# Side products of two feed-forwards: from behind a step's up products to ahead of them

## The reference, cut to what matters

```python
def conv_ffn(h, w_up, conv_w, conv_b, w_down):
    u = causal_dwconv(h @ w_up, conv_w, conv_b)
    g, up = jnp.split(u, 2, axis=-1)
    return (jax.nn.silu(g) * up) @ w_down
```

## Time and profile before

| | us |
|---|---|
| median of 3 runs | 2046.79 (2045.48 to 2047.96) |
| the profiled execution, its time | 2051.6 |
| its span | 2049.8 |
| PE busy | 2009.4 (98%) |
| DVE busy | 1330.0 (65%) |
| ACT busy | 955.7 (47%) |
| POOL busy | 159.3 (8%) |
| mean granted TensorE clock | 0.996 |

### The profile page before, as it was taken

One profiled execution on the slowest core, in us unless ns is written; L12 is line 12 of the kernel. 1 busy time (PEld: TensorE's weight loads), 2 busy tenths in 40 slices (PEclk: granted clock), 3 DMA queues, 4 the chain that ended last, 5 costly groups with the idle time before them and its releaser, 6 DMA issues.

```text
span 2049.8 us, 33452 instructions
## 1 busy us (share of the span) xinstructions
PE 2009.4 (98%) x13114; PEld 1738.3 (85%) x13114; DVE 1330.0 (65%) x2339; ACT 955.7 (47%) x1574; POOL 159.3 (8%) x169
## 2 busy tenths in 40 slices
PE   9999999999999999999999999999999999999998
PEld 7779998878999888888888788888878899888997
DVE  6767667767877337476445555868566686575665
ACT  4655555565555434353432453233246454445444
POOL 2001000000110100000200001111110000100100
PEclk9999999999999999999999999999999999999999
DMA  8446665535555322222222104534234244441554
GB/s 248 148 142 245 228 225 196 181 108 175 186 176 191 137 93 81 75 83 83 72 93 93 52 31 157 193 116 161 92 129 154 93 135 155 134 154 57 193 172 134
DMA packets 79706, 285.54 MB, mean 139 GB/s; under 512 B 8976, under 2 KB 9644, under 8 KB 79552
## 3 DMA queue, kind: packets, MB, share of 16 engines
q1 hardware_dynamic: 71136, 256.93, 37.7%
q10 hardware_dynamic: 6416, 19.51, 2.7%
q0 software_dynamic: 2000, 6.97, 1.3%
HBM read 277.55 MB, written 5.83 MB: 138 GB/s over the span
## 4 chain that ended last, share of the span: by engine, by line
PE 81%; DVE 10%; ACT 6%; issue 2%; DMA 1%; POOL 0%; ACTq 0%; DVEq 0%; SPq 0%
PE pb L1124 16%; PE pb L1126 15%; PE pb L1125 15%; PE pb L1137 6%; PE pb L1139 6%; PE pb L1138 6%; DVE SPL L2222 3%; ACT SPH L1637 3%; PE pb L1143 3%; PE pb L1302 2%; PE pb L1496 2%; PE pb L1303 2%; PE pb L1304 2%; PE pb L1477 2%; PE pb L1391 1%
## 5 line engine op out<-in xcount | busy, mean ns | idle before, releaser
L2222 DVE TENSOR_TENSOR SPL<-RAW,SPH 128x1024 fp32r<-128x1024 f32 x460 | 558.9, 1232 | 367.2 <-ACT SPH L1637 343.4
L1637 ACT ACTIVATE SPH<-RAW 128x1024 fp32r<-128x1024 f32 x462 | 477.4, 1052 | 208.4 <-PE pb L1126 111.3
L1124 PE MATMUL pb<-HTH,SPH 128*128 128x256 f32 (+1 forms) x1304 | 447.0, 343 | 8.4 <-POOL HTL L2881 3.1
L1126 PE MATMUL pb<-HTH,SPL 128*128 128x256 f32 (+1 forms) x1304 | 437.9, 336 | 0.0
L1125 PE MATMUL pb<-HTL,SPH 128*128 128x256 f32 (+1 forms) x1304 | 437.5, 335 | 0.0
L1124 PEld LDWEIGHTS pb<-HTH,SPH 128*128 128x128 f32 x1304 | 247.8, 190 | 36.8 <-ACT HTH L1686 3.2
L1126 PEld LDWEIGHTS pb<-HTH,SPL 128*128 128x128 f32 x1304 | 247.8, 190 | 26.1
L1125 PEld LDWEIGHTS pb<-HTL,SPH 128*128 128x128 f32 x1304 | 248.0, 190 | 24.8
L1137 PE MATMUL pb<-SPH,HTH 128*128 128x512 f32 x640 | 254.6, 398 | 2.1 <-DVE SPL L2222 1.4
L1139 PE MATMUL pb<-SPL,HTH 128*128 128x512 f32 x640 | 249.9, 390 | 0.0
L1138 PE MATMUL pb<-SPH,HTL 128*128 128x512 f32 x640 | 249.8, 390 | 0.0
(11 more groups left out here) (297 smaller groups left out, 2853.2 us busy)
## 6 DMA issues: line engine op xcount, KB each, us to landing
RAW<-in_w_up SPq DMA_DIRECT2D x88, 512.0 KB, 4.5
RAW<-in_wa SPq DMA_DIRECT2D x64, 512.0 KB, 3.5
RAW<-in_w_in SPq DMA_DIRECT2D x48, 512.0 KB, 4.7
RAW<-in_wmg SPq DMA_DIRECT2D x48, 512.0 KB, 3.5
RAW<-in_wbr SPq DMA_DIRECT2D x48, 512.0 KB, 3.5
RAW<-in_w_down SPq DMA_DIRECT2D x44, 512.0 KB, 4.9
RAW<-in_w_ada SPq DMA_DIRECT2D x24, 512.0 KB, 4.7
ARAW<-in_w_ada ACTq DMA_DIRECT2D x24, 512.0 KB, 4.2
```

Source lines behind the costliest of these rows:

```text
L1124: T.matmul(o, wh[:, kt, :], xh[:, kt, n0:n1], start=kt == 0, stop=False)
L1126: m = T.matmul(o, wl[:, kt, :], xh[:, kt, n0:n1], start=False, stop=kt == 7)
L1637: A.activation(hi, raw, ACT.Copy, scale=1.0).then_inc(*act.tick(s["hi"], ("u", u)))
L2222: W.tensor_tensor(lo, raw, hi.bitcast(F32), SUB).then_inc(*dve.tick(s["lo_dve"], ("u", u)))
```

## The change

In layer 0 one item of the modulation is taken at the head of steps 2 to 19, ahead of the up products, instead of behind the up products of steps 1 to 18. In layer 1 one product of the context is taken at the head of steps 8 to 15 instead of behind the up products of steps 7 to 14. ScalarE, behind its three DMAs and ahead of its wait for them, waits for VectorE's tile of ones and copies one column of it into a scratch tile.

```diff
         for j in range(FF_TILES + 2):
+            if l == 0 and 2 <= j < 20:
+                next(self.ada)
+            if l == 1 and 8 <= j < 16:
+                next(context)
             if j < FF_TILES:
...
                 self.add("up", l, j)
                 self.give(n)
-            if l == 0 and 1 <= j < 19:
-                next(self.ada)
             if j == 1 and l == 0:
...
                 context = self.products("c0", LO4)
-            if 7 <= j < 15 and l == 1:
-                next(context)
             if j == 3 and l == 1:
...
         A.dma_start(sb["PAR"][:, FIRST_PAR:], k.args["par"][:, FIRST_PAR:]).then_inc(*act.tick(s["par2"]))
+        act.wait_ge(s["const_dve"], "one")
+        A.activation(sb["SQY"][:, 0:1], sb["ONE"][:, 0:1], ACT.Copy, scale=1.0).then_inc(*act.tick(s["const_act"]))
         act.wait_ge(s["par"], 32)
```

## The result

The change made the kernel slightly slower: 2048.93 us (median of 22 runs, 2043.92 to 2053.63) against 2045.43 (22 runs, 2043.52 to 2048.28) for the kernel before. The ratio is 1.0014, with an interval of 1.0008 to 1.0020, or 1.6 to 4.1 us. I had forecast 3.5 us less.

The account below looks back on a forecast made before the run. The prediction took TensorE as the bound, 81% of the chain that ended last. Modulation -3.0, context -0.45 and tiny copy 0 made -3.5 from the runs' median 2046.8, so 2043.3 us, range 2040.0 to 2047.6.

Parts of the forecast that it names:

- The context: Second feed-forward: 8 products moved between downs and ups, each 0.44 instead of 0.50 at the slow pace; -0.45 us in all.
- hidden: VectorE's two context operations ahead of the step's splits, wanted 8.8 us later and taking 2.3, would cost TensorE nothing.
- The paces: Ups run at one of two stable paces, 276 or 281 ns per matmul, 0.20 us apart over a block of 48.
- both products give the fast pace: Rival: ups behind context products also run fast, so the context gives -2.1 and the total is 2041.7; chance 0.20.
- The modulation: First feed-forward: moved products and turns, with fast ups behind the products, give -3.0 us in all.
- turns: First feed-forward: 3 moved turns, each 0.69 at the fast pace instead of 0.93, counted at 0.23 gain each, -0.69.
- the stretch up to step 5: First feed-forward, three products included: -0.4 with a 0.6 wait for a split; bounds -1.1 and +0.6.
- its bound without a wait: The modulation's stretch up to step 5 if nothing waits: -1.1 instead of -0.4.
- The rival of late up loads: Loads landing after more than 5.1 us would delay evacuation, 1.3 in each of 11 steps: 2057; chance 0.08.
- the 1.5 to spare: First feed-forward: the next down unit would be split at 13.0, TensorE wanting it at 14.5, so 1.5 us spare.
- ScalarE's tiny copy: At the start: table load 1.28 us earlier, but TensorE still meets the first split unit at 13.26; 0, bounds -1.3 and +0.2.
- something not seen: Anywhere in the kernel: paces of later blocks shift by some 2 us in sum; chance 0.05.

Follow-up runs that it names:

- e9_mid: Against the kernel before, only the context: TensorE's product ahead of the ups, other engines' work between that step's up splits and evacuation; second feed-forward 193.9 us.
- e4: Against the kernel before, only TensorE's context products move ahead of the ups of steps 7 to 14, other engines' work stays; ratio 0.9982.
- e6: The changed kernel, but the other engines' work on the context product put back behind that step's evacuation; 2040.93 us, ratio 0.9970 to the kernel before.
- e1_mod: Against the kernel before, only the modulation's products move; ratio 0.9987.
- e7: As e6, with ScalarE's four table loads issued in step 10 of the first feed-forward instead of step 3; ratio 0.9968 to the kernel before.
- e8: As e7, with the context rows loaded in step 7 instead of 1 and spilled in step 13 instead of 6; ratio 0.9966 to the kernel before.
- e3_tiny: Against the kernel before, only ScalarE's tiny copy is added; ratio 0.9996.
- e12_mod: Against the kernel before, only the modulation's products move, run once for its trace; first feed-forward 194.8 us, second 190.0.
- e2_ctx: Against the kernel before, only the context's products move; ratio 1.0020.
- e10: The changed kernel again, nothing altered, run once for its trace; first feed-forward 195.2 us, second 194.7.
- e11: The changed kernel once more, nothing altered, run once for its trace; first feed-forward 194.5 us, second 194.7.
- e5: Against the kernel before, TensorE's context product stays behind the ups, only the other engines' work on it moves to the next step's head; ratio 1.0023.

## Why the prediction was wrong, by its own steps

**The context, the term that failed.** The prediction said that VectorE's two operations "now stand ahead of the splits of the step. These are wanted a whole step (8.8) later and take 2.3: hidden", and put the move at -0.45. It came to +4.5, where TensorE's own steps got shorter: the term failed at "hidden". Two things were missed. I added up VectorE's operations as if nothing stood between them; between them is a copy of ScalarE's, and behind that copy on ScalarE's queue stand the up units' splits. And the lead of a step was taken for slack that is there each time. It is used up once: the first two products show no wait, the third 0.16, and from then on every round is 9.64 long and the step too. The rows of the ring were all in the trace of before; what I didn't do was to walk them in the new order and set the sum against the 8.81 that I forecast for the step (8.65 where TensorE doesn't wait). e9_mid shows that such a sum can be made beforehand, once the ring is known: 9.56 against 9.54. The prediction named its own end: it falls if the two feed-forwards together don't become 1 to 6 us shorter. They became 3.4 longer.

**The paces.** The prediction took the fast pace behind the modulation's products (right: 5.57 against 5.56) and the slow one behind the context's, by the earlier trace rows (wrong: fast in all eight, 5.55 where the block is undisturbed). So of the rivals, *both products give the fast pace* was the true one as far as TensorE goes: its -2.1 for the context is e4's 188.2 against 190.0 to 190.2. The earlier trace rows was the wrong neighbour in two ways. Ahead of that product stand ups, not downs; and the pace there is not the place's own. In eleven of the fourteen profiled executions these ups are fast, in three slow (the kernel before, e4, e6), in each at the pace of the ups ahead of the products. In the changed kernel five starts take 0.57 instead of 0.59:

```profile
1549.17 0.28 PE L1125 MATMUL pb<-HTL,SPH 128*128 128x256 f32 x1
...
1549.74 0.28 PE L1124 MATMUL pb<-HTH,SPH 128*128 128x256 f32 x1
```

For the modulation's product, e1_mod answers what the prediction could not read: there the ups ahead of the first product were slow (11.50 for two blocks instead of 11.10), and the ups behind it fast (5.56).

**The modulation, the second term that failed.** It was put at -3.0 and came to -1.14. The paces and seams were right: steps of 8.97 with a product against 8.94 forecast, turns about 0.2 cheaper (0.23 forecast). What was wrong is the stretch up to step 5, forecast at -0.4 with a wait of 0.6 in it and +0.6 as the worst. It came to +1.15 in the profiled execution (40.73 instead of 39.58), with waits of 2.01. Less these waits the loop is 193.5, 3.15 under the kernel before; the sum at its bound without a wait was -3.7.

**The rival of late up loads** was right in kind and put too far off. It was to decide at a landing of 5.1; by the table above it decides near 3.7 in step 4. The difference is the 1.42 for which ScalarE issues the table loads, of the kind that I had in the earlier trace rows and had not taken off the 1.5 to spare in this rival. That is worked out from rows, and e7 and e8 agree: with the table loads in step 10 the downs of step 11 wait at landings of 3.93 and 3.86. Behind all other products of the second and third group no downs waited.

**ScalarE's tiny copy**, at 0: nothing is to be seen of it. The table load is at 2.17, the first matmul with a split unit at 13.51 (13.26 before), and e3_tiny's interval includes 1. Over all profiled executions that first matmul is at 12.4 to 13.7 with the copy and at 12.5 to 13.9 without it.

**What the profiled spans hid.** The changed kernel's span is 2.7 shorter, against +3.4 in the feed-forwards. A part of the remaining 6.1 is the wait at 62.5 (1.8 less, of which a start 0.25 later takes some back). Another is the clock, in 687 to 695 and in 1827 to 1837, at 0.79 and 0.83 before and at 1.00 after; by the starts of the same matmuls in both it is worth 1.5 and 1.6. First the kernel before, then the changed one:

```profile
687.00:695.00 8.00, 7.48 (x48) 7.34 (x49) 2.34 (x3) 4.29 (x6) 0.78 (x2) 0.79 0.77 264
...
1827.00:1837.00 10.00, 8.11 (x46) 6.87 (x46) 5.21 (x7) 2.77 (x7) 0.00 (x0) 0.83 0.63 212
```

```profile
687.00:695.00 8.00, 6.84 (x51) 6.35 (x52) 2.00 (x3) 5.99 (x10) 2.19 (x3) 1.00 0.64 224
...
1827.00:1837.00 10.00, 8.74 (x66) 7.55 (x65) 6.84 (x10) 4.40 (x10) 0.00 (x0) 1.00 0.58 213
```

The last part is the pace of a long stream of three-matmul products near 1912 to 1952, slow before and fast after at a clock of 1.00: 1.45 by the starts (groups by line, 1914 to 1950 before, 1912.7 to 1947.3 after):

```profile
L1126 PE MATMUL pb<-ABH,SPL 128*128 128x256 f32 x51 | 14.3, 281 | 0.0
...
L1126 PE MATMUL pb<-ABH,SPL 128*128 128x256 f32 x51 | 14.1, 276 | 0.0
```

That stream is fast in e1_mod and slow in e12_mod, which are the same kernel. So this is the prediction's "something not seen", shifts of later paces by some 2 us, and it belongs to the execution and not to the change.

## What to carry to other kernels

Before moving a step in a list that all engines share, walk the ring of hand-overs in the new order, engine by engine, and compare its length with the bound engine's step; here a lead of one step hid a longer ring for three rounds only. Where a product's place on TensorE is what pays, move TensorE's part alone and leave its evacuation where the other engines had it: here that turned a loss of 0.14% into a gain of 0.30%. And compare single profiled executions stage by stage, against several executions where a wait ends with a DMA.

## What the runs showed of the hardware that was not expected

Where an f32 product stands between downs and ups, the ups behind it run at the fast pace (0.113 between starts instead of 0.118): in the changed kernel's profile in all 23 places, for the modulation's products of 32 weight columns, the turns and the context's products of full width alike. It is not without exception: in e2_ctx and in both repeats of the changed kernel (e10, e11) one context block of eight was slow, each in a step that waits. Ups directly behind downs were slow, unless a wait stood between: then they were fast in five blocks of e5 (5.53) and one each of e10 and e11, slow in one each of the changed kernel and e2_ctx. What makes a block settle was not found: the first three blocks of the second feed-forward, behind the same transposes, ran slow in the kernel before (17.06 for 144) and fast in the thirteen other profiles (16.43 to 16.45).

The lower level of TensorE's clock near 690 us (in 687 to 695) appeared in five of the six profiled executions whose modulation was in the old place, and in none of the eight in which it was moved. That is about 1.5 us, and may be why e1_mod measured as much as it did; the cause was not looked for and stays open.
